# Opening of a two-block kernel: input transposed by the host and used un-normalised, one k-tile at a time

## The reference

```
h    = rms_norm(x, norm1_g)            # x * rsqrt(mean(x*x) + 1e-6) * norm1_g, per token
proj = h @ w_in                        # 1024 features -> k, v, q, gates, recurrent inputs, ...
qh   = rms_norm(heads(q), q_norm_g)    # a second norm, per head of 64
k_.. = rms_norm(heads(k..), k_.._norm_g)
```

## Time and profile before

| | before |
|---|---|
| median of 3 runs | 812.28 us (812.08 to 812.28) |
| profiled execution: span | 810.6 us |
| TensorE busy | 799.6 us, 99% of the span |
| VectorE busy | 599.4 us, 74% |
| ScalarE busy | 487.0 us, 60% |
| GpSimd busy | 27.1 us, 3% |
| DMA | 143.79 MB, mean 177 GB/s |

### The profile page before, as it was taken

The page is one execution under the profiler, slowest core; times in us unless marked ns, Lnnn a source line. Parts: engine busy times, 40 slices in busy tenths (PEclk is TensorE's granted clock), DMA queues, the critical chain, the costliest instruction groups (busy, mean ns, idle before and its releaser), DMA issues.

```text
span 810.6 us, 11913 instructions
## 1 busy us (share of the span) xinstructions
PE 799.6 (99%) x4813; PEld 693.2 (86%) x4813; DVE 599.4 (74%) x773; ACT 487.0 (60%) x738; POOL 27.1 (3%) x38
## 2 busy tenths in 40 slices
PE   8999999999999999999999999999999999999996
PEld 7889998888888888988888888888888988888885
DVE  6774698998957986897878778877777665655556
ACT  6555598877757454765666566546755654544552
POOL 1102000000000000000000000020110000000000
PEclk9999999999999999999999999999999999999999
DMA  8446432342434674456455555764453655555441
GB/s 337 164 156 251 170 126 104 118 155 73 151 119 159 229 288 156 156 188 227 160 206 174 201 197 175 256 237 147 146 196 121 211 201 196 174 219 191 161 152 52
DMA packets 22630, 143.79 MB, mean 177 GB/s; under 512 B 2608, under 2 KB 3248, under 8 KB 8240
## 3 DMA queue, kind: packets, MB, share of 16 engines
...
HBM read 141.97 MB, written 1.05 MB: 176 GB/s over the span
## 4 chain that ended last, share of the span: by engine, by line
PE 93%; ACT 3%; DVE 2%; DMA 1%; issue 1%; DVEq 0%; SPq 0%; ACTq 0%
PE PS L1748 19%; PE PS L1752 10%; PE PS L1801 10%; PE PS L1802 10%; PE PS L1805 10%; PE PS L1735 5%; PE PS L1736 4%; PE PS L1740 4%; PE PS L2115 3%; PE PS L1764 2%; PE PS L2094 2%; PE PS L1858 1%; PE PS L1892 1%; PE PS L2119 1%; PE PS L1869 1%; PE PS L2065 1%
## 5 line engine op out<-in xcount | busy, mean ns | idle before, releaser
L1074 DVE TENSOR_TENSOR WL<-RAW,WH 128x2048 fp32r<-128x2048 f32 (+2 forms) x127 | 285.1, 2247 | 31.1 <-ACT WH L629 31.0
L629 ACT ACTIVATE WH<-RAW 128x2048 fp32r<-128x2048 f32 (+2 forms) x127 | 238.2, 1877 | 47.0 <-PE PS L1805 25.7
L1490 DVE TENSOR_TENSOR HLS<-PS,HLS 128x512 f32<-128x512 f32 x46 | 31.7, 689 | 92.7 <-ACT HLS L977 92.7
L1748 PE MATMUL PS<-CHL,WH 128*128 128x512 f32 x352 | 87.9, 392 | 0.0
L1735 PE MATMUL PS<-BHL,WH 128*126 128x256 f32 (+1 forms) x336 | 83.6, 287 | 0.0
L977 ACT ACTIVATE HLS<-PS 128x512 f32<-128x512 f32 x46 | 27.4, 595 | 90.7 <-PE PS L1752 86.3
L1736 PE MATMUL PS<-BHL,WH 128*126 128x256 f32 (+1 forms) x336 | 81.8, 282 | 0.0
L1748 PE MATMUL PS<-BHL,WH 128*128 128x512 f32 x320 | 79.9, 392 | 0.0
L1748 PEld LDWEIGHTS PS<-CHL,WH 128*128 128x128 f32 x352 | 63.9, 189 | 11.8
L1802 PE MATMUL PS<-WH,AHL 128*128 128x512 f32 x176 | 68.8, 391 | 0.0
L1801 PE MATMUL PS<-WH,AHL 128*128 128x512 f32 x176 | 68.7, 390 | 0.0
...
## 6 DMA issues: line engine op xcount, KB each, us to landing
RAW<-in_w_stream SPq DMA_DIRECT2D x108, 1024.0 KB, 4.8
...
WF<-in_w_stream SPq DMA_DIRECT2D x2, 1024.0 KB, 5.4
LN<-in_ln ACTq DMA_DIRECT2D x2, 1024.0 KB, 5.2
...
```

Source lines behind the costliest of these rows:

```text
L629: eng.activation(WH[:, c % NSLOT, 0:CHUNKS[c][2]], raw(c), ACT.Copy).then_inc(w_hi, 1)
L1074: eng.tensor_tensor(WL[:, c % NSLOT, 0:CHUNKS[c][2]], raw(c), f32(WH[:, c % NSLOT, 0:CHUNKS[c][2]]), ALU.subtract).then_inc(w_lo, 1)
L1490: eng.tensor_tensor(HLS[:, n % 4, :, :], PS[:, bank:bank + 2, 0:TOK], HLS[:, n % 4, :, :], ALU.add)\
L1748: eng.matmul(PS[:, bank, :], wh, HL[:, k, :, :].rearrange("p a t -> p (a t)"), start=(k == 0), stop=False)
```

## The change

The host passes a new input `xt` besides the tokens: the norm's gain in 8 columns and the transposed tokens, 8 k-tiles x 256 tokens. It is loaded in four pieces of 256 KB between the first two weight chunks, which come in pieces of 256 and 512 KB. The k-tiles times the gain, without the roots, are split into `CH` and `CL`; the `kv` and the `q` chunks use these. The first two chunks are done one k-tile at a time. The roots come in later: as a scale at the evictions of values and squares (L796, L799, L823), and by small products on POOL into the roots of keys and queries (L620, L631). The tokens themselves, for the squares, are loaded after chunk c3 with the constants; their squares are taken in the iteration of c1.

The `cmp` and recurrence chunks still need the normed input `BH`, `BL`: after c3 TensorE spreads the roots over the partitions by two matmuls of ones with `DG` (L2120), DVE multiplies the transposed input by gain and root in place (`input_normed`, L1286), ACT copies the high part (L804), POOL subtracts for the low part (L625). Two `q` chunks are moved ahead of the `cmp` chunks to make time for this; with them goes the norm of these queries. The second keys' norm moves from c3 to c5. The matmuls on ones are 11 in place of 14. Some semaphores are merged, and some PSUM banks change; beyond c12 no engine's order is changed.

```diff
 
     out = [("kv", i, CHUNK, True) for i in range(4)]
+    out += [("q", i, CHUNK, True) for i in range(2)]
     out += [("cmp", i, CHUNK, True) for i in range(2)]
-    out += [("q", i, CHUNK, True) for i in range(4)]
+    out += [("q", i, CHUNK, True) for i in range(2, 4)]
...
-        Q_BANKS = (6, 0)
+        Q_BANKS = (0, 0)
+        CMP_BANKS = (2, 3)
+        KT_BANKS = (4, 6)
+        RS_BANK = 2
...
-                if c == 2:
-                    eng.dma_start(CN[:, P:NCONST], A_consts[:, P:NCONST]).then_inc(const_in, 16)
+                if c == 4:
+                    for t in range(NT):
+                        eng.dma_start(X0[:, t, :], A_x[t * P:(t + 1) * P, :]).then_inc(x_in[t], 16)
+                    eng.dma_start(CN[:, :], A_consts).then_inc(const_in, 16)
                     eng.dma_start(CV[:, :], A_cols).then_inc(const_in, 16)
...
                     if c == 0:
-                        first, second = slice(0, CHUNK // 2), slice(CHUNK // 2, CHUNK)
-                        eng.dma_start(raw(c)[:, first], source[:, first]).then_inc(w0_in, 16)
-                        eng.dma_start(raw(c)[:, second], source[:, second]).then_inc(raw_in[slot], 16)
+                        for n in range(2):
+                            part = slice(512 * n, 512 * n + 512)
+                            eng.dma_start(raw(c)[:, part], source[:, part]).then_inc(w0_in[n], 16)
+                        eng.dma_start(xt_pair(1), A_xt[:, KD + 2 * TOK:KD + 4 * TOK]).then_inc(xt_in[1], 16)
+                        eng.dma_start(raw(c)[:, 1024:CHUNK], source[:, 1024:CHUNK]).then_inc(raw_in[slot], 16)
+                        eng.dma_start(xt_pair(2), A_xt[:, KD + 4 * TOK:KD + 6 * TOK]).then_inc(xt_in[2], 16)
+                    elif c == 1:
+                        eng.dma_start(raw(c)[:, 0:1024], source[:, 0:1024]).then_inc(w1_in, 16)
+                        eng.dma_start(xt_pair(3), A_xt[:, KD + 6 * TOK:KD + 8 * TOK]).then_inc(xt_in[3], 16)
+                        eng.dma_start(raw(c)[:, 1024:CHUNK], source[:, 1024:CHUNK]).then_inc(raw_in[slot], 16)
...
+                power(krs[:, 8 * b:8 * b + 8], kss[:, 8 * b:8 * b + 8], 8, HD, EPS)
+                for t in range(NT):
+                    h = slice(8 * b + 4 * t, 8 * b + 4 * t + 4)
+                    eng.tensor_scalar(krs[:, h], krs[:, h], rsx[:, t:t + 1], None, ALU.mult).then_inc(k_rstd, 1)
+                if b == 0:
+                    for kp in range(4):
+                        eng.wait_ge(xt_hi, 6 + kp + 1)
+                        pair = slice(2 * kp, 2 * kp + 2)
+                        eng.tensor_tensor(BL[:, pair, :], XT[:, pair, :], f32(BH[:, pair, :]), ALU.subtract).then_inc(xt_lo, 1)
...
+                    eng.tensor_scalar(rq[:, h], rq[:, h], rsx[:, t:t + 1], None, ALU.mult).then_inc(rq_ready, 1)
             eng.wait_ge(kc_sq, 1)
...
+                        eng.activation(V[:, t, br, :], PS[:, 4 + 2 * br + t, 256:512], ACT.Copy, scale=rsx[:, t:t + 1])
                         if 2 * br + t >= 2:
...
+                    for kp in range(4):
+                        eng.wait_ge(xt_ready, 2 + kp + 1)
+                        eng.activation(BH[:, 2 * kp:2 * kp + 2, :], XT[:, 2 * kp:2 * kp + 2, :], ACT.Copy).then_inc(xt_hi, 1)
                 if kind == "cmp":
...
+
+            def first_high(k, arrived):
+                eng.wait_ge(arrived, 16)
...
+            first_high(1, w0_in[1])
+            eng.wait_ge(xt_in[0], 16)
             gained_hi(2)
             gained_hi(3)
+            first_high(2, raw_in[ARRIVAL[0][0]])
+            first_high(3, raw_in[ARRIVAL[0][0]])
+            gained_hi(4)
+            gained_hi(5)
+            first_high(4, w1_in)
+            first_high(5, w1_in)
+            gained_hi(6)
+            gained_hi(7)
+            first_high(6, raw_in[ARRIVAL[1][0]])
+            first_high(7, raw_in[ARRIVAL[1][0]])
             for c in range(NCH):
                 if c == AT["cmp", 0]:
                     eng.wait_ge(const_in, 32)
...
+            def keys_normed(br):
+                eng.wait_ge(k_rstd, NT * br + NT)
+                for t in range(NT):
+                    o = 8 * br + 4 * t
+                    src = PS[:, 4 + 2 * br + t, 0:256].rearrange("p (g d) -> p g d", g=4)
+                    eng.tensor_tensor(KN[:, br, t, :, :, :], src.unsqueeze(2).broadcast_to([P, 4, 2, HD]),
+                                      krs[:, o:o + 4].unsqueeze(2).unsqueeze(2).broadcast_to([P, 4, 2, HD]),
+                                      ALU.mult).then_inc(kn_ready, 1)
+
+            def input_normed():
+                eng.wait_ge(chunk_done, AT["kv", 3] + 1)
+                for k in range(KD):
+                    ins = eng.scalar_tensor_tensor(XT[:, k, :], XT[:, k, :], XTG[:, k:k + 1], PS[:, RS_BANK, 0:TOK],
+                                                   ALU.mult, ALU.mult)
+                    if k % 2:
+                        ins.then_inc(xt_ready, 1)
+
             def side(c):
...
+                    eng.wait_ge(xt_hi, k - 1)
+                eng.scalar_tensor_tensor(CL[:, k, :], XT[:, k, :], XTG[:, k:k + 1], f32(CH[:, k, :]), ALU.mult,
+                                         ALU.subtract).then_inc(xt_lo, 1)
+
+            def first_low(k):
+                c, n = divmod(k, 4)
+                eng.wait_ge(*high_of(k))
+                part = slice(512 * n, 512 * n + 512)
+                eng.tensor_tensor(WL[:, c, part], raw(c)[:, part], f32(WH[:, c, part]), ALU.subtract)\
+                   .then_inc(w_lo if n == 3 else w_part_lo, 1)
+
+            def x_squares():
+                for t in range(NT):
+                    eng.wait_ge(x_in[t], 16)
+                    eng.scalar_tensor_tensor(XN[:, t, 512:DM], X0[:, t, 512:DM], 1.0 / DM, X0[:, t, 512:DM], ALU.mult, ALU.mult,
+                                             accum_out=ssx[:, 2 * t + 1:2 * t + 2]).then_inc(x_sq2, 1)
+
...
+                    eng.wait_ge(x_rstd, t + 1)
+                    eng.tensor_scalar(DG[:, t, :], ident, rsx[:, t:t + 1], None, ALU.mult).then_inc(dg_ready, 1)
 
             def compressed_weights():
 
...
+            eng.memset(WARM[:, :], 1.0).then_inc(fills_ready, 1)
+            eng.memset(yeps[:, :], LN_EPS).then_inc(fills_ready, 1)
+            eng.wait_ge(xt_in[0], 16)
+            for k in range(2):
+                eng.tensor_scalar(CH[:, k, :], XT[:, k, :], XTG[:, k:k + 1], None, ALU.mult).then_inc(xt_ready, 1)
+            for k in range(KD):
+                first_low(k)
+                gained_lo(k)
             for c in range(NCH):
                 u = unit_at(c - W0)
                 if u is not None:
...
                     rg_squares(rg_group(c - W0, RG_SQUARES))
+                if c == 1:
+                    x_squares()
...
+                    roots_diagonal()
                 if CHUNKS[c - 1][:2] == ("up", N_UP - 1):
...
+                if c == 5:
+                    keys_normed(1)
                 side(c)
+                if c == 2:
+                    keys_normed(0)
                 if kind == "ri" and i:
                     rg_second(i - 1)
                 if c >= W0:
...
                     if i < 2:
-                        for kp in (2 * i, 2 * i + 1):
-                            pairs = [(t, k, slice(512 * (k % 4), 512 * (k % 4) + 512))
-                                     for t in range(NT) for k in (2 * kp, 2 * kp + 1)]
-                            eng.wait_ge((w0_half, w_hi, w_hi, w_hi)[kp], i + 1)
-                            eng.wait_ge(xt_hi, kp + 1)
...
+                            cols = slice(512 * (k % 4), 512 * (k % 4) + 512)
+                            eng.wait_ge(*high_of(k))
+                            if k < 2:
+                                eng.wait_ge(xt_ready, k + 1)
+                            else:
+                                eng.wait_ge(xt_hi, k - 1)
+                            for t in range(NT):
+                                eng.matmul(PS[:, b + t, :], CH[:, k, P * t:P * t + P], WH[:, c, cols], start=(k == 0), stop=False)
+                            eng.wait_ge(*low_of(k))
+                            for t in range(NT):
+                                eng.matmul(PS[:, b + t, :], CH[:, k, P * t:P * t + P], WL[:, c, cols], start=False, stop=False)
+                            eng.wait_ge(xt_lo, k + 1)
+                            for t in range(NT):
+                                last = eng.matmul(PS[:, b + t, :], CL[:, k, P * t:P * t + P], WH[:, c, cols], start=False,
                                                   stop=(k == KD - 1))
                                 if k == KD - 1 and t == 0:
                                     last.then_inc(tile0_done, 1)
...
-                    m = MB_NO[c]
-                    bank = mb_bank(m)
+                    bank = CMP_BANKS[i]
                     for j in range(2):
...
-            for kp in range(4):
-                for kk in range(2):
-                    k = 2 * kp + kk
```

(21 more changed lines are left out.)

208 lines of the change are left out of this document (93 added, 115 removed).

## The result

| | before | after |
|---|---|---|
| median of the runs | 812.28 us (812.08 to 812.49, 4 runs) | 817.15 us (816.17 to 818.04, 4 runs) |
| ratio, 95% interval | | 1.0059 (1.0046 to 1.0072) |
| profiled execution, span | 810.6 us | 816.2 us |
| TensorE busy in the span | 99% | 98% |

A forecast was written before the change was run, and what follows sets the result against it. TensorE, busy 99% of the span, was taken as the bound, so only the start could be won and a new wait before c12 lost. From 812.3 us, -4.4 + 0.5 + 1.0 = -2.9 gave 809.4 us, range 807.9 to 811.3.

The forecast's parts named there:

- Term 1: Opening: with squares, roots and transposes gone ahead of the first weight, c2's first matmul comes at 16.7, not 21.1: -4.4 us.
- half of it, at 376 GB/s 1.4 us earlier, by 4.6: Opening loads: the first k-tile needs 0.53 MB, half the former 1.05 MB landed at 5.97, so it is in by 4.6.
- Rival C: Opening: small pieces load slowly, at 226 GB/s, so the start isn't won; +0.8, 813.1 us; chance 7%.
- The gap before k-tile 2: Opening: TensorE idles about 0.6 us before k-tile 2, which starts at 8.35.
- Term 2: Behind c3: two added float32 matmuls on DG cost TensorE 0.47 us, taken as +0.5.
- Term 3: At c12: the chain behind the tokens readies its low part at 71.0, wanted at 70.0; +1.0 us, bounds 0 to 2.8.
- 2 us to spare against TensorE: c6's low part: ready at 38.9, wanted by TensorE at 40.9, so POOL's subtractions beside it add nothing to the sum.
- while POOL's own L600 kept 1.28 an instruction: POOL and DVE working at once: DVE's low part takes 3.06 us for 2.29, while POOL isn't slowed.
- I charge nothing for the clock: Opening: TensorE's gaps of about 0.6 us cost no clock, since earlier idling from 6.1 to 7.47 kept 1.00.
- upper bound of 2.8: Wait at c12 if tokens and c5 land 1 us later and POOL's work also slows DVE once; time 811.2 us.
- D: Token squares: tokens land 7.9 us late, holding DVE's queue and weight loads; +5.0, 817.3 us; chance 7%.
- Slower: Outcome above 813.9 us, from rival D and a bit of rival C; chance 0.08.

The follow-up runs named there:

- the kernel with the lowest time: Kernel after, with constants' chain and first keys' norm later, fills and first KT in DVE's gaps, c0's first half loaded as one piece: 809.66 us.

## Why the prediction was wrong, by its own steps

**Term 1, the opening: right in kind, -3.0 for -4.4.** The first matmul was expected at 5.0 to 5.6 and came at 6.42. The step that failed: "half of it, at 376 GB/s 1.4 us earlier, by 4.6". The loads ran at 275. The first weights landed at 5.50 and the first input at 5.92 (expected 4.6), k-tile 2 began at 9.59 (8.35), and c2 landed at 16.07 (14.3). Rival C was dismissed because 512 KB pieces had run at 376, while six of the opening's nine pieces, half of its bytes, were of 256 KB; and even 512 KB pieces ran at 300 to 308 at this place. C's mechanism was there, at 1.4 of the 4.7 us it had there. The gap before k-tile 2 didn't appear, as TensorE came later itself.

**Term 2:** right, +0.5.

**Term 3, the chain behind the tokens, is the step that turned the sign.** The wait was named at the right place, for DVE, and "nearly unbroken" from c8's low part on: 14.39 us (54.17 to 68.56) for the 14.4 forecast. Its size was 3.87 for 1.0. The last `QN` ended at 74.85, where the text had 68.8; the 6.0 come from:
- the start of c3's low part, 21.65 for 19.6: +2.0. The second token half landed at 21.0 for 18.9, but it was not alone: c2, itself late by the slow loads, kept DVE at its low part until 20.3, and DVE stood idle for only 0.1 us at the squares;
- the keys' norm of the first pair, which stands ahead of c5's low part on DVE and waits for POOL. The list went from c5's high part straight to its low part. +1.7, and 0.2 in c5's load (c5's high part ended at 30.89, the low part began at 32.59). The run with the norm moved shows it;
- c6's low part 3.11 for 2.29 beside POOL's instructions: +0.8. The text knew this row and gave it 2 us to spare against TensorE. There were none, as the wait of 0.64 at c6 shows. And the part is also a link in the chain to `QN`, where a delay isn't absorbed by such slack;
- keys and roots up to the first `QN`s +1.0, the last sums and roots +0.4. A pass of roots with the product is 2.45, not 2.25, and handing over comes on top.

That the wait is on `QN`, ahead of c12's high part, and not on its low part 1.95 later, was wrong too, though both came out near 1 us.

**Wrong in direction: "while POOL's own L600 kept 1.28 an instruction".** The text took from the earlier trace rows that DVE pays beside POOL. In those rows POOL had begun first; they can't show what POOL pays when DVE begins first. For the roots it is POOL that pays. The Trainium skill says so (SBUF — State Buffer, SBUF: two separate sides): the shared ports are "an exclusive lock", and whichever starts first holds them for its whole instruction, when DVE has two SBUF inputs and POOL reads from SBUF. POOL's 2.76 for 0.39 agrees, and so does the run with the roots first, 0.64. In the run with the keys' norm moved POOL even waited through two DVE instructions in a row, 3.85 for 0.3.

**"I charge nothing for the clock".** Right for the opening, where the clock stayed at 1.00. It was not asked of the new wait, where it cost some 2.5 us: nearly half of the shift at the end. With the wait at its upper bound of 2.8 the text still had 811.2; at this place single executions with waits of 0.85, 2.69 and 2.96 kept the clock, and those with 3.44, 3.86 and 3.87 lost it. So a wait somewhat longer than the range allowed cost more than its own length.

**The rivals.** D's number (817.3) is that of the result, and its mechanism is partly that: the tokens and c3's low part come late, and all behind them in DVE's queue. But its condition, a landing at 23.4 or later, wasn't met (about 21.0), and DVE hardly stood at the squares. Two thirds of the lateness of `QN`, 4.0 of 6.0 us, came from links further down, and 2.5 of the time from the clock. That D's number came out is luck. "Slower" had 0.08.

**What held.** The shift at c12 was kept to the end, DVE was what c12 waited for, and the sum without term 3 is what the kernel with the lowest time shows: c2 -3.56 (17.60 against 21.16), `DG` +0.48, c12 -3.04 (68.89 against 71.93), no wait, -2.7 us in time.
